# One layer pair with an RWKV recurrence on one core: the k and v projections of the tile after next are moved from between the recurrence steps to the projections in front of the triangular inverse

## The reference

```python
(na_q, na_k, na_v, na_gate, pool_u, pool_gate, rw_r, rw_k, rw_v, rw_gate,
 rw_lw, rw_la, merge_logits) = jnp.split(h @ w_in, IN_SPLIT_POINTS, axis=-1)
...
def step(S, inp):
    rt, vt, wt, kt, at, bt = inp
    sa = jnp.einsum('bhij,bhj->bhi', S, at)
    S = S * wt[:, :, None, :] + sa[..., None] * bt[:, :, None, :] + vt[..., None] * kt[:, :, None, :]
    return S, jnp.einsum('bhij,bhj->bhi', S, rt)
```

## Time and profile before

| | us |
|---|---|
| Median of 3 runs | 3904.54 (3903.04 to 3904.77) |
| The profiled execution, its time | 3903.8 |
| The profiled execution, its span | 3902.0 |
| PE busy, share of the span | 3715.8, 95% |
| DVE busy | 1568.7, 40% |
| ACT busy | 679.2, 17% |
| POOL busy | 191.5, 5% |
| Mean granted TensorE clock, 1 is 2.4 GHz | 0.979 |

### The profile page before, as it was taken

How to read it: one execution, slowest core, us unless ns; L and a number is a source line. 1 busy time by engine, 2 the same in 40 slices (tenths; PEclk the granted TensorE clock), 3 DMA queues, 4 the chain that set the end, 5 groups by cost and what they waited for, 6 DMA issues and landing times. The chain is left out here.

```text
span 3902.0 us, 68453 instructions
## 1 busy us (share of the span) xinstructions
PE 3715.8 (95%) x30322; PEld 2816.8 (72%) x30322; DVE 1568.7 (40%) x3045; ACT 679.2 (17%) x1614; POOL 191.5 (5%) x267
## 2 busy tenths in 40 slices
PE   5999999998998999999999999999999987999998
PEld 3688745555787676788748778566666666999998
DVE  1323343653334232212200541355555555665565
ACT  1100122420002122212100220122222221000001
POOL 0000000000000000000000000021122222000000
PEclk9999999999999999999999999999999997999999
DMA  8543223223542532355333334211111100444442
GB/s 337 217 161 142 109 97 119 87 87 115 209 159 79 214 129 73 146 216 206 139 137 142 110 108 146 94 35 47 36 41 41 47 35 24 152 163 165 179 175 110
DMA packets 73526, 490.17 MB, mean 126 GB/s; under 512 B 8448, under 2 KB 10496, under 8 KB 19472
## 3 DMA queue, kind: packets, MB, share of 16 engines
q1 hardware_dynamic: 70560, 462.45, 32.4%
q0 software_dynamic: 2672, 23.35, 1.5%
HBM read 481.57 MB, written 4.19 MB: 124 GB/s over the span
## 5 line engine op out<-in xcount | busy, mean ns | idle before, releaser
L1137 PE MATMUL ps<-h,w 128*128 128x256 f32 (+1 forms) x2816 | 930.0, 475 | 19.6 <-ACT h L1806 14.4
L1137 PEld LDWEIGHTS ps<-h,w 128*128 128x128 f32 x2816 | 522.7, 193 | 284.8 <-issue 234.2
L1243 PE MATMUL ps<-h,w 128*128 128x256 f32 (+1 forms) x1024 | 370.2, 500 | 1.3 <-issue 1.3
L1243 PEld LDWEIGHTS ps<-h,w 128*128 128x128 f32 x1024 | 182.4, 189 | 90.2 <-issue 69.3
L1402 PE MATMUL ps<-zone 64*64 64x64 f32 x4608 | 174.4, 221 | 22.6 <-DVE zone L2492 20.8
L2208 DVE TENSOR_TENSOR modc<-ps,bmod 128x4 f32<-128x4 f32 x72 | 11.4, 159 | 429.2 <-PE ps L1085 428.5
L1545 PE MATMUL ps<-h,zone 128*128 128x128 f32 (+1 forms) x1328 | 180.6, 289 | 0.0
L1402 PEld LDWEIGHTS ps<-zone 64*64 64x64 f32 x4608 | 156.4, 135 | 33.3 <-ACT zone L1927 24.0
L1545 PEld LDWEIGHTS ps<-h,zone 128*128 128x128 f32 x1328 | 167.6, 192 | 6.0 <-issue 1.6
L1077 PE MATMUL ps<-w,zone 128*32 128x256 f32 x2304 | 148.7, 401 | 23.8 <-DVE zone L2668 11.7
L1131 PE MATMUL ps<-w,h 128*128 128x256 f32 x768 | 168.6, 380 | 0.0
(11 more groups left out here) (443 smaller groups left out, 5176.7 us busy)
## 6 DMA issues: line engine op xcount, KB each, us to landing
w<-in_wm SPq DMA_DIRECT2D x144, 1024.0 KB, 6.6
w<-in_w SPq DMA_DIRECT2D x48, 1024.0 KB, 4.9
w<-in_we SPq DMA_DIRECT2D x36, 1024.0 KB, 5.0
w<-in_wi SPq DMA_DIRECT2D x34, 1024.0 KB, 4.9
w<-in_wrw SPq DMA_DIRECT2D x32, 1024.0 KB, 5.0
w<-in_wo SPq DMA_DIRECT2D x24, 1024.0 KB, 5.4
w<-in_wmg SPq DMA_DIRECT2D x24, 1024.0 KB, 6.6
w<-in_wbr SPq DMA_DIRECT2D x48, 512.0 KB, 4.6
```

The source lines that it names most:

```text
L1137: last = mm(pass_psum(s, q), rows[:, n * P:(n + 1) * P], src[k], start=(k == 0), stop=(k == s.kt - 1))
L1243: last = mm(ps[:, m, 0:T - NC * n], halves.rows(k)[:, m * P:(m + 1) * P], h[:, k, NC * n:T], start=(k == 0), stop=(k == KT - 1))
```

## The change

On PE, `rw_recur` loses its `passes` argument and all its fills. `rw_invert` of tile `it` gets both groups of projections, one behind the other: passes 2 and 3 of tile `it+1`, then passes 0 and 1 of tile `it+2`. On ACT, the two copies of passes 2 and 3 move from round 12 and from behind the last round to a place ahead of the rounds. ACT's copies of passes 0 and 1 stay where they were, at step 4 and at the end of the steps. Nothing else is edited: the order of the weight panels, DVE's, POOL's and SP's programs stay.

```diff
@@ PE, rw_recur @@
-            def rw_recur(it, passes=iter(()), feed=None):
-
-                def fill(n):
-
-                    for _ in range(n):
-                        next(passes, None)
+            def rw_recur(it, feed=None):
...
-                    fill(2)
                     pe.wait_ge(s_w1e, 8 * it + i + 1)
...
-                    fill(1)
                     pe.wait_ge(s_ue, 8 * it + i + 1)
...
-                    fill(1)
                 if feed is not None:
                     rw_bonus_sum(feed)
-                for _ in passes:
-                    pass
@@ PE, the loop over the tiles @@
             for it in range(8):
-                rw_invert(it, rw_passes(it + 1, (2, 3)) if it < 7 else iter(()))
-                rw_recur(it, rw_passes(it + 2, (0, 1)) if it < 6 else iter(()), it + 1 if it < 7 else None)
+                ahead = [(it + 1, (2, 3))] if it < 7 else []
+                if it < 6:
+                    ahead.append((it + 2, (0, 1)))
+                rw_invert(it, (step for at, xs in ahead for step in rw_passes(at, xs)))
+                rw_recur(it, it + 1 if it < 7 else None)
@@ ACT, rw_invert @@
                 if it >= 1:
                     rw_square(it - 1)
+                if it < 7:
+                    rw_raw(it + 1, 2)
+                    rw_raw(it + 1, 3)
                 for n in range(20):
...
-                    if n == 12 and it < 7:
-                        rw_raw(it + 1, 2)
                 if it < 7:
-                    rw_raw(it + 1, 3)
                     rw_norm_square(it + 1)
```

## The result

The changed kernel takes 4009.33 us (median of 4, 4004.89 to 4010.32), the kernel before 3903.79 us (median of 4): a ratio of 1.0271, 95% interval 1.0258 to 1.0284, so 2.7% slower. The forecast was 4005 us with a range of 3984 to 4032.

A forecast was written before the change was run, and what follows sets the result against it. PE was taken to bound the filled steps, a PE-DVE chain the unfilled ones. Per tile 27.5 - 13.8 + 2.6 + 0.4 = 16.7 us, six tiles 100 us, on 3904.54: forecast 4005 us, range 3984 to 4032.

The forecast's parts named there:

- The main term: Tiles: packed k and v projections ahead of the inverse add 27.5 us bare on PE, unfilled steps give back 13.8.
- tile 6 is the changed kernel in small: Steps of tiles 0 to 5 become like tile 6's unfilled ones: 34.37 us instead of 48.17.
- The signs named beforehand: Profile: 128 projection instructions in one run of about 41 us, steps 33 to 36, tiles about 121, mean clock about 0.96.
- The clock term: Start of the next tile, six times: PE begins at half clock, 2.6 us more, plus 0.4 us a tile.
- The 0.4: Added per tile, in us, for a low clock running into the projections or coming earlier in the steps.
- Covers costed at nothing: Copies on ACT, preparations of other engines and panel fetches stay hidden beside PE's work: 0 us.
- ACT's copies: Copies of passes 2 and 3 ahead of the rounds: 0, at most 0.8 us a tile either way.
- Weight panels: SP's fetches of k and v panels land before use: cost 0; a late half would bare up to 5 us.
- A: Clock holds at 2.4 GHz in unfilled steps: a tile costs 9.7 us, 3963 us in all; chance 0.08.
- B: Clock stays low well into the projections or falls as early as in tile 7: 5.1 us a tile, 4036; chance 0.11.
- C: No slower: packing saves 6.1 us a tile of PE time if steps shrink, deciding at 20.7 us; 3868; chance 0.03.
- D: Ahead of the rounds, PE waits for a panel half or ACT's copies: up to 5 us a tile, 4035; chance 0.04.

The follow-up runs named there:

- the shortened passes: The changed kernel with 3 matmuls instead of 16 in each moved k or v pass of tiles 2 to 7: 3873.60 us.
- the doses: Against the kernel before, only part of the 32 k and v matmuls moved ahead of the inverse: the k pass 3925.46 us, 8 matmuls 3903.31 us.

## Why the prediction was right

**The main term held.** 27.5 us a tile were to be added and 13.8 to go. Added: 83.47 us in an inverse at the high clock against 55.92, which is 27.55. Gone: 49.03 to 36.0 us on average, 13.0. The step that tile 6 is the changed kernel in small was right to a tenth for half of the tiles; the others lie 1.4 us above, with a short drop of the clock ahead of the long one. The signs named beforehand came as well: one run of 128 instructions in 41.45 us, a mean clock of 0.955, and tiles of 122.6 to 123.1 us where 121 were named.

**The clock term was right in its place and small by what it left out.** 2.6 + 0.4 us a tile were taken, and 2.7 were measured at the start of tiles 1 to 6. The 0.4 stood for an earlier fall or a low clock in the projections. The first cost 0.7 us a tile in the steps, because tile 6 had been read from one trace in which its short drop is missing; that is 4 us in six tiles, and 1.3 more in tile 6 itself. So the clock took 21.5 us where 18 were summed. That is most of the gap between 100 us forecast and 105.5 measured; the idle stretches of PE in the inverses of tiles 2 and 5 are 2 us more of it. That the trace read beforehand showed the shorter of two lengths was bad luck, and a small one.

**Covers costed at nothing were nothing.** ACT's copies: shown in the kernel before by that part alone. Preparations beside the packed part: shown by the shortened passes, which gave back 135.7 of 134 us. Weight panels: not tried by themselves, but PE has no wait in the 41.45 us of projections, and with the clock held the inverse is 55.92 + 27.55.

**The rivals.** A (the clock holds) did not happen. Holding it by idle matmuls gave 11 us, not 42: the tile's start came back, the 4 us a tile in the steps did not. The changed kernel's own steps say why in part: one late step takes 4.87 us at either clock, while an early one loses 1.4 us to a drop. What all steps together would take at the high clock without idle matmuls stays open. In tile 7, where DVE has 10.9 us of work and not 26.6, the clock gave 4.4 us. B did not happen: the clock was back at 2762.4, before that tile's first projection at 2762.7, and so in all six tiles; only the earlier fall that B also names showed, as the short drop. C is refuted by the changed kernel itself, whose steps of 35.2 to 36.8 us are far above the 20.7 where it would have begun; the doses show that the steps stop shrinking in proportion between 24 and 16 matmuls. D did not show.

**The Trainium skill's two rules.** The Trainium skill (TensorE: Matmul & The Clock Gate, "HAM oscillation") has the loss at half of the throttled time. With 27.3 us a tile that would be, as an estimate by that rule, 13.7, and 82 us in six tiles, to be had by holding the clock; 11 us came back. At the start of a tile, where PE is dense, the rule fits: 5.9 us at 1.2 GHz cost 2.7. In the late step above it doesn't: 4.87 us at either clock. The idle matmuls' own cost is in the 11 us, so the whole isn't measured cleanly here. Its other rule, that it takes long gaps for the clock to fall, disagrees with six more stages: it fell in each, with single waits of PE of 1.8 us at most in tile 2 and 2.4 us in tile 4.

## What to carry to other kernels

Work that fills waits is free only up to the point where the filling engine becomes the bound. What lies beyond that point costs the same in the stage or outside it (24 or 32 matmuls: no difference), and what lies below it costs more outside than it frees (from 24 to 16, 6.9 us for 3.3; from 16 to none, 13.7 us for 2.9). Compare the stage with fills, without, and the filler's own busy time before moving anything. A loop whose last rounds already run without the filler shows the changed kernel in the trace of the old one; look at more than one trace of it, as its length can differ from run to run (35.2 to 37.0 us here). And when a stage has waits, look for work from behind it to put in, not for work to take out.

## What the runs showed of the hardware

The stage of tile 7 got shorter by taking on work: 16 more instructions and 3.9 us less, with PE at 2.4 GHz for most of it; with 16 idle matmuls instead it was 4.4 us less at a clock of 1.00. In the changed kernel the low clock reached from the steps into the next tile's first matmuls, 5.9 us in tile 0, and the steps took 35.3 us without or 36.7 us with a short drop of 3.4 us ahead of the long one. A step whose chain waits for DVE took 4.87 us at 0.50, at 0.71 and at 1.00 of the clock. Steps with 16 fills, PE busy 34.7 of 38.9 us, never lost the high clock.
